# A two-block network kernel on one Trainium2 core: the scan's helper work is placed elsewhere, and the odd layer's half exchange goes from TensorE to DMA

## The chip, the core and the metric

The kernel runs on one core of a Trainium2 chip. The core has four engines that compute: TensorE (PE in the profile, its weight loads are PEld), VectorE (DVE), ScalarE (ACT) and GpSimd (POOL). SyncE (SP) issues most transfers. Each engine runs its own instructions in order and waits on semaphores for the others. The metric is the time of one execution on the device in microseconds (us).

## What is computed

The reference runs a first network of two layers (feed-forward blocks around two mixers), and then a second one of an even and an odd layer, on 512 latent tokens and 256 context tokens of width 1024, all in float32. The change touches two places of the second network. In the even layer a recurrence runs over the tokens, forwards and backwards, in 12 heads of 64:

```python
def step(s, inp):
    r_t, w_t, k_t, v_t, kk_t, b_t = inp
    sa = jnp.einsum('bhij,bhj->bhi', s, kk_t)
    s = s * w_t[:, :, None, :] - sa[..., None] * b_t[:, :, None, :] + v_t[..., None] * k_t[:, :, None, :]
    return s, jnp.einsum('bhij,bhj->bhi', s, r_t)
```

In the odd layer q and k of each of 8 heads of width 128 are turned by a position-dependent angle, which pairs feature d with feature d + 64:

```python
t1, t2 = t[..., :half], t[..., half:]
return jnp.concatenate([t1 * cos - t2 * sin, t1 * sin + t2 * cos], axis=-1)
```

## The kernel before, in words

Activations lie with features on the partitions and tokens in the free dimension (768 columns: 512 latent, 256 context). Weights come in chunks of 512 KB by SP; ACT makes a rounded copy of each (`w_hi`, L258), GpSimd the rest (`w_lo`, L266), and TensorE multiplies with both (L303).

**The even scan** (`even_scan_phase`). The 12 heads are done two at a time, in 6 blocks. A block has 6 steps, one for each 128 tokens, and a step does both directions d = 0 and 1. For each 128 tokens the recurrence is turned into products with a triangular 128x128 matrix that must be inverted. Three kinds of work run at once, all placed by hand in the in-order programs of the engines:

- The *step* of block b: `chunk_parts` (`take`, `keys`, `cross`, `join`, `turn`, `close`, for the step to come) and `state_parts` (`right`, `solve`, `read`, `write`, for this step). DVE masks and adds (`br`, `kqr`, `y`, `x`, then `add`, L2884 to L2891), ACT copies out of PSUM. ACT's first copy of a step is `bq` (L2681); its start marks the step in this document.
- The *inversion* of block b+1: its diagonal 32x32 blocks are gathered by DMA to 96 partitions, and GpSimd runs 30 rounds of substitution (`invert`, L2321 to L2331). ACT then writes a turned (transposed) copy in two pieces, L2667 for the first 21 columns and L2671 for the rest. SP writes both forms to DRAM (`scatter`, L2236 and L2239) and reads them back as `image` (L2259), which `cross` of the block needs (L2455).
- The *preparation* of block b+2: from the projected rows it makes the decays, their powers, and their products with r, k and so on (`prepare` on each engine).

Preparation and inversion are cut into slots: a block has 36, six in each step, and `between(slot)` in a step places slot n = 6k + slot (first the inversion's part, then the preparation's). The slots that matter: the reciprocals of the key norm `inv` (128 columns each, L2805) stand at n = 9 to 14; ACT's powers at n = 17 to 26; the turned copies at n = 25 and 27; DVE's `rk` (L2824) at n = 28; DVE's copy of the last decay column and its product with the row r (`last`, L2829, and `r`, L2832) at n = 29 and 30; `bonus` (L2837), which waits for `r1`, at n = 32; the lower triangles for the inversion (`low`, PE L2420, DVE L2940) at n = 33, 34, 35 and at 0, 1, 2 of the next block. GpSimd does the inversion of c and then the ten products of the preparation of c+1 (L2338): `kk`, `ksum`, `bkk0`, `b0`, `q0`, `bkk1`, `b1`, `q1`, `kw0`, `kw1`; `kk` waits for `inv`. Blocks 0 and 1 are prepared ahead of the first step, the others inside steps: blocks 0 to 3 of steps hold a preparation, block 4 holds only the inversion of block 5, and block 5 holds nothing. Where blocks are numbered below it is the block whose steps run, from 0 to 5, and steps are 0 to 5 too.

**The odd layer** (`odd_phase`). For each head h TensorE does `project(h, Q)`, `turn_values(h-1)`, `project(h, KEY)`, `rotate(h, Q)`, `turn_keys(h-1)`, `project(h, V)`, `rotate(h, KEY)`, `products(h-1)`, `project(h-1, G)`, `outputs(h-1)`. ACT copies each result out (`evacuate`: `plain` for q and k, L3304 and L3309), and `project(h, V)` waits for the copy of KEY, since both use the bank `con`. `rotate` (L3426) is a product with a 128x128 matrix of 0, 1 and -1 that swaps the halves. DVE's `turn` then forms plain x cos + rotated x sin in three operations (L3535, L3536, L3538). `products` and `outputs` wait for ACT and DVE in their turn.

## Time and profile before

| | us |
|---|---|
| median of 3 runs | 3448.47 |
| lowest, highest | 3445.60, 3452.94 |
| the profiled execution | 3458.49 |
| its span, first to last instruction | 3456.7 |
| PE busy | 3143.7 (91%) |
| DVE, ACT, GpSimd busy | 1642.9, 1177.2, 1317.2 |
| mean granted TensorE clock | 0.945 |
| the scan's steps, first to last | about 2440 to 2902 |
| the odd layer | about 3043 to the end |

The span is the time from the first to the last instruction of one profiled execution; the time outside it is 1.8 us. Busy shares are means over the whole program. What an edit is worth is read from the stage in which it stands.

### The profile page before, as it was taken

How to read it: one execution, taken by the hardware profiler on the slowest of the kernel's cores; microseconds unless marked ns; L12 is line 12 of the kernel's file. 1: busy time of each engine (PE TensorE's matmuls, PEld its weight loads, DVE VectorE, ACT ScalarE, POOL GpSimd, SP SyncE). 2: the span in 40 equal slices, each digit the busy share in tenths (PEclk: the TensorE clock that was granted, in tenths of full speed). 3: DMA queues.
4: the chain of work that ended last, by engine and by line, in shares of the span. 5: the costliest groups of instructions: out<-in, count | busy, mean ns of one | idle time of the engine just before them, and what ended most of it. 6: DMA issues, size and time to landing. Idle time of an engine off the chain costs nothing. (4 is left out here: it accounts for less than half of the span.)

```text
span 3456.7 us, 51217 instructions
## 1 busy us (share of the span) xinstructions
PE 3143.7 (91%) x19551; PEld 2512.9 (73%) x19551; DVE 1642.9 (48%) x3075; ACT 1177.2 (34%) x2107; POOL 1317.2 (38%) x863
## 2 busy tenths in 40 slices
PE   6999989799998999989899989996788889979996
PEld 5888865588886888767688867874566666758875
DVE  6444377344535573332531115426777755264443
ACT  2222235322223222234322223234444434243342
POOL 3444431344443434333344432224666630133332
PEclk8999989899998999989899999997899999979998
DMA  7565421265544554322333332222222233112111
GB/s 228 180 188 165 133 66 48 74 194 184 165 155 129 179 167 140 110 74 62 119 109 95 96 94 85 63 93 64 47 54 55 55 104 108 37 54 62 56 49 43
DMA packets 633361, 361.15 MB, mean 104 GB/s; under 512 B 106830, under 2 KB 626756, under 8 KB 632672
## 3 DMA queue, kind: packets, MB, share of 16 engines
q1 hardware_dynamic: 628960, 351.48, 34.3%
q10 hardware_dynamic: 3056, 6.29, 0.5%
q8 instruction: 124, 2.03, 0.2%
q0 software_dynamic: 1168, 0.91, 0.1%
q14 instruction: 53, 0.43, 0.0%
HBM read 333.73 MB, written 24.90 MB: 104 GB/s over the span
## 5 line engine op out<-in xcount | busy, mean ns | idle before, releaser
L266 POOL TENSOR_TENSOR w_lo<-w_raw,w_hi 128x1024 fp32r<-128x1024 f32 (+1 forms) x398 | 940.4, 2364 | 1731.9 <-ACT w_hi L258 1731.9
L303 PE MATMUL acc<-h,w_hi 128*128 128x512 f32 x3136 | 979.0, 393 | 6.7 <-POOL w_lo L266 6.7
L258 ACT ACTIVATE w_hi<-w_raw 128x1024 fp32r<-128x1024 f32 (+1 forms) x398 | 414.5, 1042 | 989.2 <-PE acc L303 961.0
L303 PEld LDWEIGHTS acc<-h,w_hi 128*128 128x128 f32 x3136 | 584.2, 188 | 128.6 <-POOL w_lo L266 7.8
L303 PE MATMUL acc<-h,w_lo 128*128 128x512 f32 x1568 | 613.4, 391 | 0.0
L303 PE MATMUL acc<-hid,w_hi 128*128 128x512 f32 x1408 | 437.3, 392 | 0.0
L303 PE MATMUL lat<-h,w_hi 128*128 128x512 f32 x912 | 336.6, 408 | 19.6 <-DVE h L429 17.6
L303 PEld LDWEIGHTS acc<-h,w_lo 128*128 128x128 f32 x1568 | 294.9, 188 | 63.6
L830 DVE SCALAR_TENSOR_TENSOR ada_part<-ada_raw,c_act,ada_part 128x256 f32<-128x256 f32 x672 | 314.9, 488 | 18.6
L303 PEld LDWEIGHTS acc<-hid,w_hi 128*128 128x128 f32 x1408 | 263.7, 188 | 54.2
L303 PE MATMUL acc<-hid,w_lo 128*128 128x512 f32 x704 | 275.2, 391 | 0.0
L1162 DVE TENSOR_TENSOR prod<-sil,acc 128x512 f32<-128x512 f32 x88 | 60.5, 688 | 420.1 <-ACT sil L1074 400.7
L303 PEld LDWEIGHTS lat<-h,w_hi 128*128 128x128 f32 x912 | 172.7, 192 | 66.0 <-issue 13.4
L353 DVE TENSOR_TENSOR ssq<-ssq,sq 128x512 f32<-128x512 f32 (+1 forms) x41 | 44.4, 1084 | 301.2 <-ACT sq L455 270.3
L303 PE MATMUL con<-h,w_hi 128*128 128x256 f32 x656 | 186.0, 284 | 0.0
L303 PE MATMUL lat<-h,w_lo 128*128 128x512 f32 x456 | 183.0, 401 | 0.0
L303 PEld LDWEIGHTS acc<-hid,w_lo 128*128 128x128 f32 x704 | 132.5, 188 | 28.0
L303 PEld LDWEIGHTS con<-h,w_hi 128*128 128x128 f32 x656 | 125.4, 191 | 0.1
L1165 DVE TENSOR_TENSOR hid<-prod,hid 128x512 f32 (+1 forms) x88 | 67.8, 771 | 81.6 <-ACT hid L1076 81.6
L2058 DVE SCALAR_TENSOR_TENSOR u<-lat,mods,u 128x504 f32 (+1 forms) x80 | 56.7, 708 | 99.7 <-ACT u L1962 96.7
L303 PEld LDWEIGHTS lat<-h,w_lo 128*128 128x128 f32 x456 | 87.4, 192 | 22.0
L323 PE MATMUL acc<-h,w_hi 128*128 128x512 f32 x192 | 71.4, 457 | 23.1 <-DVE h L570 23.1
(517 smaller groups left out, 4844.5 us busy)
## 6 DMA issues: line engine op xcount, KB each, us to landing
w_raw<-in_ffn_w SPq DMA_DIRECT2D x240, 512.0 KB, 3.9
ada_raw<-in_ada_w SPq DMA_DIRECT2D x88, 1024.0 KB, 4.9
w_raw<-in_od_w_in SPq DMA_DIRECT2D x32, 512.0 KB, 4.0
w_raw<-in_ev_w_in SPq DMA_DIRECT2D x30, 512.0 KB, 3.8
w_raw<-in_ffn_w SPq DMA_DIRECT2D x32, 384.0 KB, 3.3
image<-inverse_wait SPq DMA_DIRECT2D x144, 64.0 KB, 2.1
first_ada<-in_ada_w SPq DMA_DIRECT2D x8, 1024.0 KB, 12.5
w_raw<-in_ab_w_in SPq DMA_DIRECT2D x16, 512.0 KB, 3.8
```

The source lines that it names most:

```text
L258: act.activation(K.w_hi[:, first % SPLIT, 0:tiles, :], K.raw[:, first % RAW, 0:tiles, :], ACT.Copy).then_inc(K.hi_ready, 1)
L266: pool.tensor_tensor(K.w_lo[:, first % SPLIT, 0:tiles, :], K.raw[:, first % RAW, 0:tiles, :], K.w_hi[:, first % SPLIT, 0:tiles, :].bitcast ...
L303: mm = pe.matmul(out, w[:, slot, k, :], moving(ap, k, tokens), start=first and k == 0 and p == 0, stop=last and k == tiles - 1 and p == le ...
L323: mm = pe.matmul(outs[c], w[:, (n + c) % SPLIT, kc, :], moving(ap, kc, LAT), start=kc == 0 and p == 0, stop=kc == DB - 1 and p == len(PASS ...
L353: dve.tensor_tensor(K.ssq[:, 0:width], K.ssq[:, 0:width], K.sq[:, b % 2, 0:width], ALU.add).then_inc(N.ssq_added, 1)
L830: ins = dve.scalar_tensor_tensor(out, raw[:, k, :], col, part[:, v, :], ALU.mult, ALU.add)
L1162: dve.tensor_tensor(prod[:, s % 2, :], sil[:, s % 2, :], banks[2 * (s % 2) + 1][:], ALU.mult).then_inc(S.prod_ready, 1)
L1165: dve.tensor_tensor(hid[:, LO, at(i, 1), :], prod[:, s % 2, :], hid[:, HI, at(i, 1), :].bitcast(F32), ALU.subtract).then_inc(S.hid_ready, 1)
L2058: dve.scalar_tensor_tensor(dst, src, col, dst, ALU.mult, ALU.add).then_inc(S.shifted, 1)
```

## The change

In the scan:

- The turned copies move from n = 25 and 27 to n = 20 and 23 (for all blocks but the first).
- `r0` and `r1` go from DVE to GpSimd: for the blocks 2 to 5 behind `q0`, for the blocks 0 and 1 behind `q1`. `last0` and `last1` go from DVE to ACT, both at n = 28. ACT's powers stand one slot later (24 to 27). `bonus` waits for GpSimd's `r1`.
- For the blocks 2 to 5 the six reciprocals stand at n = 9, 10, 11, 19, 21 and 22 (9 to 14 before), and `inv` is signalled at the last of them.

In the odd layer the 16 matrix products are gone. Behind the copy-out and the split of q and of k, ACT waits for its own copy and issues two DMAs that write the upper half of `plain` to the lower half of `swapped` and the other way round; DVE waits for their landing, and its first operation now reads SBUF where it read PSUM. The sign is in the table `rope`, and the 64 KB load of `rot` is gone.

```diff
 PREP = {
-    "act": [..., "q0", "q1", "w0", "w1"],
-    "dve": ["kk", "max", "sum0", "inv", "sum1", ..., "before1", "rk", "last0", "r0", "last1", "r1", "bonus"],
-    "pool": ["kk", "ksum", "bkk0", "b0", "q0", "bkk1", "b1", "q1", "kw0", "kw1"],
+    "act": [..., "q0", "q1", "w0", "w1", "last0", "last1"],
+    "dve": ["kk", "max", "sum0", "sum1", ..., "before0", "inv", "before1", "rk", "bonus"],
+    "pool": ["kk", "ksum", "bkk0", "b0", "q0", "r0", "r1", "bkk1", "b1", "q1", "kw0", "kw1"],
...
+                        if d == (c < 2):
+                            for e in range(2):
+                                op(f"r{e}", O.cs[e], O.cs[e], reads, ALU.mult, ("act", f"last{e}"))
...
+                        if n == 28:
+                            act.wait_ge(S.pa, prep("act", c, f"w{d}"))
+                            t = 0 if d else CH - 1
+                            act.activation(O.wlast[:, d, :], O.cs[d].rearrange("p (c t) -> p c t", t=CH)[:, :, t],
+                                           ACT.Copy).then_inc(S.pa, 1)
...
-                    if c and n == 25:
+                    if c and n == 20:
                         act.wait_ge(S.solving, c * (2 * N - 2) + 2 * early)
...
-                    if n == (27 if c else 17):
+                    if n == (23 if c else 17):
                         act.wait_ge(S.solved, c + 1)
...
+                    places = (9, 10, 11, 19, 21, 22) if c > 1 else range(9, 15)
...
                     if n == 32:
-                        own("r1")
+                        dve.wait_ge(S.pq, prep("pool", c, "r1"))
...
                     split(n + SPLIT)
+                    if kind in (Q, KEY):
+                        act.wait_ge(S.evac, n + 1)
+                        for to, of in ((slice(0, 64), slice(64, 128)), (slice(64, 128), slice(0, 64))):
+                            act.dma_start(swapped[kind][to], halves(plain[of, kind, :])).then_inc((S.q_swapped, S.k_swapped)[kind], 16)
...
-                    rotate(h, Q)
...
-                    rotate(h, KEY)
...
-                    dve.wait_ge(S.rot_ps, 2 * h + kind + 1)
+                    dve.wait_ge((S.q_swapped, S.k_swapped)[kind], 32 * h + 32)
...
-                    steps(dve.tensor_tensor(part[:], rot_ps[:], rope[:, 1, :], ALU.mult))
+                    part = swapped[kind]
+                    steps(dve.tensor_tensor(part, part, halves(rope[:, 1, :]), ALU.mult))
```

Where the order of instructions moves, three places. On DVE at the join of step 4 and step 5 of a block with a preparation (`state` ends step 4; `br` and `kqr` are `take` and `keys` of step 5), before:

```order
L2891 SCALAR_TENSOR_TENSOR state<-gathered,w_last,const 128x128
L2824 SCALAR_TENSOR_TENSOR x_context<-x_context,params,u 128x768
L2829 COPY w_last<-q_r_rate 128x6
L2832 TENSOR_TENSOR q_r_rate<-q_r_rate,u 128x768
L2848 TENSOR_TENSOR br<-chunk_479,masks 128x256
L2848 TENSOR_TENSOR br<-chunk_493,masks 128x256
L2829 COPY w_last<-q_r_rate 128x6
L2832 TENSOR_TENSOR q_r_rate<-q_r_rate,u 128x768
L2855 TENSOR_TENSOR kqr<-chunk_479,masks 128x512
```

and after:

```order
L2892 SCALAR_TENSOR_TENSOR state<-gathered,w_last,const 128x128
L2833 SCALAR_TENSOR_TENSOR x_context<-x_context,params,u 128x768
L2849 TENSOR_TENSOR br<-chunk_479,masks 128x256
L2849 TENSOR_TENSOR br<-chunk_493,masks 128x256
L2856 TENSOR_TENSOR kqr<-chunk_479,masks 128x512
```

The four instructions of `last` and `r` between the step's own are gone. On ACT at the end of step 3 of such a block (`sa` is `solve`, `t` and `y` are `turn` and `close`, `q_r_rate` a power, `bq` opens step 4), before:

```order
L2711 ACTIVATE sa<-state_494 128x128
L2689 ACTIVATE t<-chunk_479 64x2x64
L2692 ACTIVATE y<-chunk_479 64x128
L2689 ACTIVATE t<-chunk_493 64x2x64
L2692 ACTIVATE y<-chunk_493 64x128
L2698 ACTIVATE t<-chunk_479 64x2x64
L2698 ACTIVATE t<-chunk_493 64x2x64
L2623 ACTIVATE q_r_rate<-q_r_rate 128x768
L2681 ACTIVATE bq<-chunk_479 128x256
```

and after:

```order
L2718 ACTIVATE sa<-state_494 128x128
L2674 ACTIVATE w_raw<-w_raw 96x32x21
L2696 ACTIVATE t<-chunk_479 64x2x64
L2699 ACTIVATE y<-chunk_479 64x128
L2696 ACTIVATE t<-chunk_493 64x2x64
L2699 ACTIVATE y<-chunk_493 64x128
L2705 ACTIVATE t<-chunk_479 64x2x64
L2705 ACTIVATE t<-chunk_493 64x2x64
L2678 ACTIVATE w_raw<-w_raw 96x32x11
L2688 ACTIVATE bq<-chunk_479 128x256
```

The two pieces of the turned copy (`w_raw`) came from behind the `sa` of step 4; the second stands ahead of the `bq` of step 4 now. In block 4, which has no preparation, the order is the same without the power. On ACT in the odd layer, from the copy-out of q to that of k (`v_tok` and `k_zeta` are tokens of the head before, `var` and `m` belong to the output of the one before that), before:

```order
L3304 ACTIVATE plain<-lat_631 128x512
L258 ACTIVATE w_hi<-w_raw 128x1024
L3322 ACTIVATE v_tok<-factors_498 128x512
L3326 ACTIVATE v_tok<-factors_499 128x256
L3329 ACTIVATE k_zeta<-factors_499,zeta 128x128 x4
L3350 ACT_TABLE_LOAD
L3350 ACTIVATE var<-var 128x512
L3354 ACTIVATE m<-sq 128x512
L3308 ACTIVATE k<-con 128x256
L3309 ACTIVATE plain<-lat_632 128x512
```

and after:

```order
L3303 ACTIVATE plain<-lat_631 128x512
L254 ACTIVATE w_hi<-w_raw 128x1024
L3321 DMA swapped<-plain 64x512 x2
L3325 ACTIVATE v_tok<-factors_498 128x512
L3329 ACTIVATE v_tok<-factors_499 128x256
L3332 ACTIVATE k_zeta<-factors_499,zeta 128x128 x4
L3353 ACT_TABLE_LOAD
L3353 ACTIVATE var<-var 128x512
L3357 ACTIVATE m<-sq 128x512
L3307 ACTIVATE k<-con 128x256
L3308 ACTIVATE plain<-lat_632 128x512
```

The row of the two DMAs is new there; two more stand behind the split that follows the copy-out of k.

## Rows read from the trace of the kernel before

**Rows 1.** Windows: start:end length, busy PE PEld DVE ACT POOL, clock, DMA share, GB/s.
```profile
2823.10:2833.30 10.20, 9.85 (x168) 7.73 (x167) 5.44 (x16) 5.89 (x18) 4.97 (x14) 1.00 0.25 39
2833.30:2849.20 15.90, 11.79 (x169) 9.29 (x167) 5.54 (x16) 3.84 (x17) 0.00 (x0) 0.89 0.39 76
...
3131.70:3321.80 190.10, 188.40 (x1070) 159.23 (x1070) 87.48 (x100) 73.42 (x121) 62.97 (x30) 1.00 0.20 56
```

**Rows 2.** Windows: steps 4 and 5 together, of blocks 0 to 3.
```profile
2493.90:2526.50 32.60, 26.84 (x363) 21.02 (x361) 23.98 (x42) 11.85 (x38) 18.84 (x10) 0.84 0.28 57
2579.80:2611.40 31.60, 24.16 (x362) 18.70 (x361) 23.94 (x42) 11.83 (x37) 18.88 (x10) 0.95 0.29 59
2665.00:2696.90 31.90, 25.44 (x362) 19.97 (x361) 23.86 (x43) 11.85 (x38) 18.20 (x9) 0.89 0.26 54
2750.10:2780.30 30.20, 24.22 (x363) 18.57 (x361) 23.89 (x42) 11.84 (x38) 18.82 (x10) 0.94 0.30 62
```

**Rows 3.** Timeline (start, length, instruction, wait), DVE and PE, block 2, step 5.
```profile
2675.73 1.78 DVE L2829 COPY w_last<-q_r_rate 128x6 f32<-128x6 f32 x1
2677.55 2.52 DVE L2832 TENSOR_TENSOR q_r_rate<-q_r_rate,u 128x768 f32<-128x768 f32 x1
...
2680.65 1.11 DVE L2829 COPY w_last<-q_r_rate 128x6 f32<-128x6 f32 x1
2681.79 2.52 DVE L2832 TENSOR_TENSOR q_r_rate<-q_r_rate,u 128x768 f32<-128x768 f32 x1
...
2684.96 1.29 PE L2455 MATMUL chunk<-image,bq 64*64 64x64 f32 x16 [2.76 <-DVE kqr L2855]
```

**Rows 4.** Timeline of GpSimd, block 2: preparation behind the inversion.
```profile
2662.87 1.82 POOL L2338 TENSOR_TENSOR x<-x,x_context 128x768 f32<-128x768 f32 x1 [0.18 <-POOL w_raw L2329]
...
2671.08 3.65 POOL L2338 TENSOR_TENSOR q_r_rate<-q_r_rate,x 128x768 f32<-128x768 f32 x2
...
2677.44 1.80 POOL L2338 TENSOR_TENSOR q_r_rate<-q_r_rate,x 128x768 f32<-128x768 f32 x1
```

**Rows 5.** One line's instructions (min/median/max ns, first to last): DVE's reciprocals.
```profile
L2805 DVE RECIPROCAL x_context<-x_context x36: 893/935/954, 2322.6 to 2730.6; 128x128 f32<-128x128 f32 x36
```

**Rows 6.** Timeline of ACT and PE, block 4: steps 4 and 5.
```profile
2823.08 0.38 ACT L2681 ACTIVATE bq<-chunk 128x256 f32<-128x256 f32 x1 [1.38 <-PE chunk L2439]
...
2829.18 0.82 ACT L2671 ACTIVATE w_raw<-w_raw 96x352 f32<-96x352 f32 x1 [1.11 <-POOLq L2331]
...
2839.84 0.45 PE L2455 MATMUL chunk<-image,bq 64*64 64x64 f32 x8 [3.15 <-DMA image<-inverse_wait]
```

**Rows 7.** Timeline of GpSimd, DVE and PE just ahead of block 0.
```profile
2427.94 1.79 POOL L2338 TENSOR_TENSOR q_r_rate<-q_r_rate,x 128x768 f32<-128x768 f32 x1
...
2430.58 1.02 DVE L2837 TENSOR_TENSOR u<-prep,u 128x512 f32<-128x512 f32 x2
...
2431.75 1.23 PE L2420 MATMUL prep<-q_r_rate 64*128 64x128 f32 x8 [7.86 <-DVE u L2837]
```

**Rows 8.** Timeline of ACT and PE, odd layer, one head: KEY to V.
```profile
3254.78 0.63 ACT L3354 ACTIVATE m<-sq 128x512 fp32r<-128x512 f32 x1 [4.94 <-DVE sq L3573]
...
3255.51 1.02 PE L3426 MATMUL rot<-plain,rot 128*128 128x512 f32 x2
...
3255.99 0.59 ACT L3309 ACTIVATE plain<-lat 128x512 f32<-128x512 f32 x1
...
3256.37 0.60 PE L3454 MATMUL factors<-const,k 128*128 128x128 f32 x4
...
3256.72 0.47 PE L303 MATMUL lat<-h,w_hi 128*128 128x512 f32 x1
```

**Rows 9.** ACT behind a DMA issue; its landing (us, last); PE, head 1.
```profile
2309.59 1.06 ACT L258 ACTIVATE w_hi<-w_raw 128x1024 fp32r<-128x1024 f32 x1 [0.46 <-ACT late L1885]
...
late_wait<-late ACTq DMA_DIRECT2D x10, 384.0 KB, 2.3
...
3104.61 0.47 PE L303 MATMUL lat<-h,w_hi 128*128 128x512 f32 x1 [1.45 <-ACT plain L3309]
```

More of the change, by code:

```diff
@@ L157, in constants @@
     cos, sin = np.cos(ang), np.sin(ang)
-    rope = np.stack([np.concatenate([cos, cos]), np.concatenate([sin, sin])]).astype(np.float32)
-    rot = np.zeros((P, P), np.float32)
-    for d in range(half):
-        rot[half + d, d] = -1.0
-        rot[d, half + d] = 1.0
+    rope = np.stack([np.concatenate([cos, cos]), np.concatenate([-sin, sin])]).astype(np.float32)
     posrow = np.stack([np.broadcast_to(i + 1.0, (P, P)), np.broadcast_to(P - i + 0.0, (P, P))])
@@ L166, in constants @@
         "dft_feat": feat.astype(np.float32), "dft_ctx": time[0], "dft_lat": time[1],
-        "rope": rope, "rot": rot, "posrow": posrow.astype(np.float32),
+        "rope": rope, "posrow": posrow.astype(np.float32),
     }
@@ L2080 @@
     "pe": ["norm", "decay0", "decay1", "rate0", "rate1", "bonus"],
[3 rows of a table removed]
-}
[3 rows of a table added]
+}
+PREP_FIRST = dict(PREP, dve=["kk", "max", "sum0", "inv", "sum1", "kt0", "kt1", "k0", "k1", "before0", "before1", "rk", "bonus"],
+                  pool=["kk", "ksum", "bkk0", "b0", "q0", "bkk1", "b1", "q1", "r0", "r1", "kw0", "kw1"])
 SUBBLOCK = 32
@@ L2166, in prep @@
         def prep(engine, c, name):
[L2168 removed]
+            return c * len(PREP[engine]) + ((PREP if c > 1 else PREP_FIRST)[engine].index(name) + 1)
         def blocks(prepare, invert, low, begin, step):
@@ L2340, in prepare @@
                     q, rate = O.q, O.rate
+                    reads = u[:, c:c + 1, :].rearrange("p a t -> p (a t)")
                     op("kk", kk, kk, tmp, ALU.mult, ("dve", "inv"))
@@ L2752, in _ @@
                 late(1)
-                for n in range(17, 25):
+                for n in range(17, 26):
                     prepare(0, n)
                 late(2)
-                for n in range(25, NCH * SLOTS):
+                for n in range(26, NCH * SLOTS):
                     prepare(0, n)
@@ L2801, in prepare @@
                         done(dve.tensor_scalar(tmp, tmp, 1e-12, None, ALU.max))
-                    if 9 <= n < 15:
+                    places = (9, 10, 11, 19, 21, 22) if c > 1 else range(9, 15)
+                    if n in places:
                         own("max")
-                        sl = slice((n - 9) * CH, (n - 8) * CH)
+                        part = places.index(n)
+                        sl = slice(part * CH, part * CH + CH)
                         inverse = dve.reciprocal(tmp[:, sl], tmp[:, sl])
+                        if part == NCH - 1:
+                            done(inverse)
                     if 11 <= n < 15:
                         sums((n - 11) % 2, (n - 11) // 2)
-                    if n == 14:
-                        done(inverse)
                     for d in range(2):
@@ L2824, in prepare @@
                         done(dve.scalar_tensor_tensor(tmp, tmp, col("r_k"), row(0), ALU.mult, ALU.mult))
-                    for d in range(2):
-                        if n == 29 + d:
-                            act(f"w{d}")
-                            t = 0 if d else CH - 1
-                            done(dve.tensor_copy(O.wlast[:, d, :], O.cs[d].rearrange("p (c t) -> p c t", t=CH)[:, :, t]))
-                        if n == 29 + d:
-                            own(f"last{d}")
-                            done(dve.tensor_tensor(O.cs[d], O.cs[d], row(0), ALU.mult))
                     if n == 32:
-                        own("r1")
+                        dve.wait_ge(S.pq, prep("pool", c, "r1"))
                         dve.wait_ge(S.pp, prep("pe", c, "bonus"))
@@ L3211, in odd_phase @@
     with phase(K, *norm_names("pre"), *norm_names("post"), *SUB_SEMS, "tables", "logits", "decay_tables", "lg", "steps",
-               "decays", "made", "evac", "rot_ps", "rot_read", "roped", "turned", "turn_copied", "sc_ps", "sc_ready",
+               "decays", "made", "evac", "q_swapped", "k_swapped", "rot_read", "roped", "turned", "turn_copied", "sc_ps", "sc_ready",
                "kv_ps", "states", "xi_ready", "o_ps", "o_copied", "sum_ps", "var", "std", "inv", "m_full", "m_hi",
@@ L3223, in odd_phase @@
         rope = S.sb("rope", [P, 2, SEQ])
-        rot = S.sb("rot", [P, P])
         plain = S.sb("plain", [P, 2, SEQ])
-        part = S.sb("part", [P, SEQ])
+        halves = lambda ap: ap.rearrange("p (a t) -> p a t", a=2)
+        swapped = (halves(S.sb("swapped", [P, SEQ])), K.sq[:, :, SEQ:TOK])
         q = S.sb("q", [P, 2, SEQ])
@@ L3260, in _ @@
                 sp.dma_start(rope[:], A["rope"].rearrange("m p t -> p m t")).then_inc(S.tables, 16)
-                sp.dma_start(rot[:], A["rot"]).then_inc(S.tables, 16)
                 sp.dma_start(lg[:, 5, :], A["od_decay_logit_2"].rearrange("a d h -> a (d h)").broadcast_to(
@@ L3420, in project @@
                              before=(lambda k: pe.wait_ge(S.h_ready, k + 1)) if n == 0 else None)
-                def rotate(h, kind):
-                    pe.wait_ge(S.evac, number[h, kind] + 1)
-                    if h or kind:
-                        pe.wait_ge(S.rot_read, 2 * h + kind)
-                    pe.matmul(rot_ps[:], rot[:], plain[:, kind, :], start=True, stop=True).then_inc(S.rot_ps, 1)
                 def piece(t, h, c):
@@ L3481, in sums @@
                     pe.matmul(R[1][:], K.ones, K.ssq[:], start=True, stop=True).then_inc(S.sum_ps, 1)
-                pe.wait_ge(S.tables, 32)
                 for h in range(HEADS):
@@ L3525, in _ @@
                         "spread")
-                dve.wait_ge(S.tables, 32)
+                dve.wait_ge(S.tables, 16)
                 def turn(h, kind):
                     dst = (q, k)[kind][:, h % 2, LAT]
-                    dve.wait_ge(S.rot_ps, 2 * h + kind + 1)
+                    dve.wait_ge((S.q_swapped, S.k_swapped)[kind], 32 * h + 32)
                     if h >= 2:
```

8 lines of the change are left out of this document (3 added, 5 removed), and 4 rows, old and new, of the table PREP.

## The prediction

> **What bounds the kernel now.** I read the windows first, to see which stages the change touches and what is busy there; then the waits and the timeline of the scan's longest steps; then the timeline of one head of the odd layer. The chain of waits of the page covers only the last microseconds and says nothing on these stages.
>
> A step of block 4 with nothing but the last of an inversion in it takes 10.2 us, of which PE is busy 9.85 [rows 1]: a bare step is bound by PE and by short hand-overs. Of the steps that hold a preparation, 4 and 5 are the longest pair: together 32.6, 31.6, 31.9 and 30.2 us in the four blocks [rows 2], 31.6 in the mean, where two bare steps are 20.4. In them DVE is busy 24 us of 32, and the preparation's work stands ahead of the step's: in step 5 `last` and `r` take 1.78 + 2.52 us, then comes `br`, then they take 1.11 + 2.52 us, and only then comes `kqr`, for which PE waits 2.76 us [rows 3]. The granted clock of these windows is 0.84 to 0.95 [rows 2] against 1.00 in the bare step [rows 1]; PE had idled just before it fell.
>
> The odd layer's steady part has PE busy 188.4 of 190.1 us at clock 1.00 [rows 1]. It is bound by PE, or by what stands just behind it.
>
> **Scan, `last` and `r` off DVE (blocks 0 to 3).** The four instructions are 1.78 + 2.52 + 1.11 + 2.52 = 7.9 us of DVE [rows 3], all on the path of step 5. They are not 7.9 us of gain, for PE is next: the four windows hold 24.2 to 26.8 us of PE, the larger ones at the lower clock [rows 2]. At full clock I put PE's work at 23.5 us. Above that stand the hand-overs, which in a bare step are 0.35 us (10.2 less 9.85), so 0.7 for two, and the three `low` products of step 5, where PE waits in turn for DVE's mask: some 2 us (an estimate). That is a floor of about 26. The new load of GpSimd gives back something: two products at 1.82 us each [rows 4] make its preparation 3.6 us longer, so that it now overlaps nearly all of step 5. I take 27 us for the pair, against 31.6: **-4.5 us a block, -18 in all**. Bounds: 25.6 (-24 in all) and 29.6 (-8).
>
> The row for the giving back: a product of 768 columns on DVE took 2.52 us, from 2677.55 to 2680.07 [rows 3]; a GpSimd product ran from 2677.44 to 2679.24 [rows 4], and DVE was done 0.83 us behind its end. The Trainium skill (SBUF — State Buffer, Who interferes with whom) states that a DVE instruction with two SBUF inputs and a GpSimd one exclude each other for their whole length. By that rule the two `state` updates in step 5 can each wait up to one GpSimd product, so the pair would be up to 3.6 us longer in each block and the scan's gain -3.6 instead of -18; this pair of rows agrees with the rule. GpSimd worked through most of step 5 before the change too, so I count little of it.
>
> ACT takes `last` at n = 28 behind its powers, two copies of six columns, where the turned copies (the second piece alone 0.82 us [rows 6]) leave step 4: nothing on the path. `r0` waits for it. GpSimd's `r1`: `kk` starts at 2662.87 in block 2, the inversion having just ended [rows 4]; with `inv` now signalled at the end of step 3 I put it 1.2 us later. The two products from 2671.08 on are `q0` and `bkk1` [rows 4], so `q0` ended at 2672.9 and now ends at 2674.1, `r1` at 2677.8. `bonus` would be reached in step 5 about 3.5 us behind the step's start of 2675.9, so near 2679. It fits by little more than a microsecond; a late `r1` would hold DVE and behind it `x`, `state` and the `low` masks.
>
> **Scan, the reciprocals.** Three of 0.94 us [rows 5] leave step 2 and come into step 3. Step 2 is bound by DVE and gains 2.8; step 3 has small slack on DVE (some 0.5 us) and pays 2.3. Less PE idling in step 2 may help the clock there and hurt it in step 3. Sum **0**, bounds -3 and +4 over four blocks.
>
> **Scan, the turned copy.** In blocks 0 to 3 it stands at the end of step 3, where the inversion has just ended (2662.87 less 0.18 [rows 4]; step 4 starts at 2665.0). The power that stood at n = 23 has moved on and makes room. The images come earlier, but PE does not wait for them there. **0**. In block 4 steps are bare, and the inversion ends late: ACT's second copy had to wait for it until 2829.18 although it stood in the middle of step 4 [rows 6]. Now it stands ahead of `bq` of step 4, which was at 2823.08 [rows 6]: ACT is held until 2829.18 + 0.82 = 2830.0, and step 4 starts 6.9 us late. The copy is no earlier than before, so the images land no earlier, at 2839.84. But step 5 then reaches `cross` near 2843 and waits no more; it lost 15.9 - 10.2 = 5.7 us before [rows 1]. Net 6.9 - 5.7 = 1.2, and PE idles twice as long at a stretch, which costs clock: **+2 us** (0 to +5).
>
> **Ahead of block 0.** `bonus` of block 1 ran at 2430.58, and PE waited 7.86 us for it [rows 7]. Now it waits for `r1`, behind `q1`, which ended at 2427.94 + 1.79; without DVE's products in its way 0.5 earlier, 2429.2; two products of 1.82: 2432.8. **+2.3 us** (+1 to +3). `kw0` and `kw1` move later behind it, and the first steps do not need them.
>
> **Odd layer.** A rotation holds PE 3256.37 - 3255.51 = 0.86 us [rows 8], 16 of them 13.8. They do not all come back. Behind `rotate(h, Q)` and the 0.35 us of `turn_keys` stands `project(h, V)`, at 3256.72, and it needs the copy of KEY, which ended at 3255.99 + 0.59 = 3256.58 [rows 8]: that rotation was covered but for 0.14. And ACT gets longer just there. An issue put 0.46 us between two of its instructions [rows 9]; two stand between the copy of q and the value tokens, some 0.8 us, and I let a short wait of ACT for PE take 0.25 of it. All behind it, `var`, DVE's reciprocal and `m` (ending at 3255.41 [rows 8]) move by 0.55, to 3255.96. The copy into `k` ahead of `plain` stood at 3255.7, so it starts 0.25 later, and V starts 0.25 us *later* than before. The rotation of KEY, between V and `products`, comes back whole: what `products` waits for was ready long before. So a steady head gives 0.86 - 0.25 = 0.6 us; seven KEY rotations give 6.0, six heads of the other kind cost 1.5. Heads 0 and 1 are tied to ACT (PE waited 1.45 us for it at 3104.61 [rows 9]); there the rotation of KEY of head 0 no longer holds DVE's decay tables up, and with ACT's issues I put it at -1.6. Sum **-6 us**. Bounds: -13.8 if every rotation comes back, and +1 if an issue pair holds ACT for 1.6 us.
>
> The transfers themselves: a landing took 2.3 us [rows 9]; DVE uses q and k more than 5 us after, behind its other work. The first of `turn`'s operations now reads SBUF twice. Covered: PE needs the result only one projection later.
>
> **The sum.** -18 + 0 + 2 + 2.3 - 6 = -19.7. The profiled execution was 3458.5 and would be 3438.8; it lay 10 us above the median of the three runs, so for the median 3448.5 - 19.7 = **3429 us**.
>
> **Rivals.** (a) *The exchange frees all it removed, and the pair comes down to PE's floor*: ACT's issues fall into its waits. For it: ACT is busy 73 of 190 us there [rows 1]. Against it: the rows that follow each other from q's copy to k's. 3448.5 - 13.8 - 24 + 4.3 = 3415. (b) *GpSimd and DVE hold each other up*: the pair gives 2 us a block only. For it: 2.52 against 0.94. 3448.5 - 8 + 4.3 - 6 = 3439. The rule above is this rival; by its full length it would be 3443. (c) *The changes in the scan do nothing, since steps 4 and 5 are bound by PE at the low clock*: PE busy 26.8 of 32.6 at 0.84 [rows 2]. Against it: the waits for DVE come ahead of the low clock. Gain 0 there: 3448.5 + 4.3 - 6 = 3447. (d) *Slower: GpSimd's `r1` is the new end of step 5.* It is ready 1.2 us ahead of `bonus` by my count. Each microsecond it is late holds DVE, and with it `x` and the `low` masks, in four blocks. From 6 us late on, 4 x 6 = 24 us have eaten the gain; at 9 us late it is 3429 + 36 = 3465. Against it: GpSimd would need some 23 us for the seven products to `r1`, and two took 3.65 [rows 4].
>
> **Chances.** The forecast 0.53, (a) 0.17, (b) 0.19, (c) 0.07, (d) 0.04. The median of this kernel can be told from no change from about 0.2% on, 7 us. Faster by more than that, under 3441.6: the forecast, (a) and most of (b), 0.87. Within: 0.09. Slower: 0.04. The range that should hold 8 in 10 leaves out (c), (d) and the far half of (a): 3412 to 3442.
>
> **What would show it.** Right: the two steps 4 and 5 of block 2 together near 27 us, with no `last` or `r` row on DVE and PE's wait for `kqr` under 1 us; step 2 shorter and step 3 longer by the same; ACT waiting some 7 us for the inversion's end in block 4, step 3, and no wait for `image` in step 5; a wait of PE for `plain` ahead of each V of about 1 us, and none for `swapped`; a head at 37.4 us for 38.0. Wrong: `bonus` waiting for GpSimd; `state` rows over 1 us in step 5; a head at 36.3 (rival a) or over 38.

## The result, and the profile after the change

The changed kernel's median is 3431.0 us (four runs, 3429.75 to 3433.30). The kernel before, run beside it, is at 3450.7 us (3445.60 to 3455.39). The ratio is 0.9945, 95% interval 0.9931 to 0.9959: 19.7 us less. The prediction was 3429.0, or 19.7 us less than its own median of before. In a later comparison on another occasion the changed kernel was at 3436.79 against 3448.87 (ratio 0.9955, 0.9943 to 0.9968), so the gain is 12 to 20 us by two comparisons, and in both it is more than the 0.2% (7 us) from which on a change can be told.

The profiled executions have spans of 3456.7 and 3431.5 us, 25.2 apart. 5.8 of these lie ahead of the scan's first step, in code that the change does not touch. The rest divides as follows. Steps are marked by the start of ACT's first `bq`, heads of the odd layer by the start of ACT's copy of `gates`, in both traces.

| part | before | after | difference | predicted |
|---|---|---|---|---|
| ahead of block 0 (wait for `bonus`) | 30.2 | 32.3 | +2.2 | +2.3 |
| steps 4 and 5, blocks 0 to 3 | 126.2 | 106.5 | -19.7 | -18 |
| step 2, blocks 0 to 3 | 66.6 | 56.9 | -9.7 | -11 |
| step 3, blocks 0 to 3 | 43.2 | 49.0 | +5.8 | +9 |
| steps 0 and 1, blocks 0 to 3 | 104.6 | 107.7 | +3.1 | 0 |
| block 4, its six steps | 68.9 | 71.6 | +2.7 | +2 |
| odd layer, six steady heads | 228.2 | 222.7 | -5.4 | -3.7 |
| odd layer, first heads and the rest | | | +1.8 | -2.3 |

The predicted -11 and +9 are the prediction's 2.8 and 2.3 us for four blocks; in its sum it booked the two together as 0.

Windows of the changed kernel, the columns of [rows 1]. First the four pairs of steps 4 and 5, which answer to [rows 2]:

```profile
2489.71:2516.27 26.56, 23.57 (x362) 18.17 (x361) 18.30 (x39) 10.75 (x38) 22.51 (x12) 0.97 0.35 72
2568.98:2596.26 27.28, 24.29 (x362) 18.77 (x361) 18.29 (x39) 10.74 (x38) 22.50 (x12) 0.94 0.38 78
2649.91:2675.75 25.84, 22.84 (x362) 17.77 (x361) 18.30 (x39) 10.76 (x39) 22.50 (x12) 1.00 0.33 67
2729.32:2756.10 26.78, 24.15 (x362) 18.76 (x361) 17.76 (x38) 10.97 (x39) 21.49 (x12) 0.93 0.36 70
```

DVE is busy 18 us in place of 24, GpSimd 22.5, and the pair takes 26.6 us in the mean for 31.6.

Then block 4, steps 3, 4 and 5, and five steady heads of the odd layer, which answer to [rows 1]:

```profile
2788.91:2805.58 16.67, 11.22 (x193) 8.72 (x191) 5.65 (x16) 6.04 (x19) 13.61 (x28) 0.97 0.01 2
2805.58:2817.52 11.94, 10.27 (x141) 8.22 (x142) 5.48 (x16) 3.86 (x17) 0.00 (x0) 0.75 0.63 110
2817.52:2827.65 10.13, 9.87 (x168) 7.67 (x167) 5.44 (x16) 3.81 (x16) 0.00 (x0) 1.00 0.13 30
3138.65:3324.25 185.60, 181.01 (x1052) 155.84 (x1051) 77.62 (x100) 74.09 (x120) 59.49 (x29) 1.00 0.25 69
```

Step 3 is now the long one, step 4 runs at clock 0.75 behind it, and step 5, which took 15.9 us in [rows 1], takes 10.1 like any bare step. A head takes 37.12 us for 38.03.

The timeline of ACT at the end of block 4's step 3 (start, length, instruction, idle before it and what ended that): the second turned copy waits 6.87 us for the inversion's end, where [rows 6] had 1.11.

```profile
2804.76 0.80 ACT L2678 ACTIVATE w_raw<-w_raw 96x352 f32<-96x352 f32 x1 [6.87 <-POOLq L2329]
```

The timeline of DVE in block 2 around the start of step 5 (2660.63), which answers to [rows 3], and of GpSimd there, which answers to [rows 4]:

```profile
2659.52 2.57 DVE L2833 SCALAR_TENSOR_TENSOR x_context<-x_context,params,u 128x768 f32<-128x768 f32 x1
2662.01 0.74 DVE L2849 TENSOR_TENSOR br<-chunk,masks 128x256 f32<-128x256 f32 x2
2664.44 1.29 DVE L2856 TENSOR_TENSOR kqr<-chunk,masks 128x512 f32<-128x512 f32 x2 [1.69 <-PE chunk L2448]
...
2666.49 1.01 DVE L2838 TENSOR_TENSOR u<-prep,u 128x512 f32<-128x512 f32 x2
...
2670.11 1.08 DVE L2892 SCALAR_TENSOR_TENSOR state<-gathered,w_last,const 128x128 f32<-128x128 f32 x1
```

```profile
2657.59 1.86 POOL L2336 TENSOR_TENSOR q_r_rate<-q_r_rate,x 128x768 f32<-128x768 f32 x1
2659.41 4.34 POOL L2336 TENSOR_TENSOR q_r_rate<-q_r_rate,u 128x768 f32<-128x768 f32 x2
2663.72 1.82 POOL L2336 TENSOR_TENSOR q_r_rate<-q_r_rate,x 128x768 f32<-128x768 f32 x1
```

No `last` and no `r` stands on DVE. DVE now waits for PE ahead of `kqr`, and PE no longer waits for `kqr` (2.76 us before). GpSimd's `r0` and `r1` (2659.41, two) are ready at 2663.75, 2.7 us ahead of `bonus` (2666.49), which waits for nothing. But `rk` (L2833) takes 2.57 us and the first `state` 1.08. Before, in the same block, they took:

```profile
2674.80 1.00 DVE L2824 SCALAR_TENSOR_TENSOR x_context<-x_context,params,u 128x768 f32<-128x768 f32 x1
...
2692.37 0.35 DVE L2891 SCALAR_TENSOR_TENSOR state<-gathered,w_last,const 128x128 f32<-128x128 f32 x1
```

The same instruction has two durations. That is the thread of what follows.

Ahead of block 0, DVE, which answers to [rows 7]; PE waits 10.03 us there for 7.86:

```profile
2426.95 1.02 DVE L2838 TENSOR_TENSOR u<-prep,u 128x512 f32<-128x512 f32 x2 [11.91 <-POOL q_r_rate L2336]
```

### The profile page after: what moved, and what is told of

Same layout as the page of the kernel before. It is cut to its first block and busy times, and to the rows that moved or that the text cites. A ratio compares the mean times of both kernels' runs of the same rounds, so it can differ in the third digit from the quotient of the medians.

```text
span 3431.5 us, 51169 instructions
## 1 busy us (share of the span) xinstructions
PE 3121.0 (91%) x19519; PEld 2497.9 (73%) x19519; DVE 1591.0 (46%) x3051; ACT 1180.3 (34%) x2119; POOL 1330.3 (39%) x875
## 5 line engine op out<-in xcount | busy, mean ns | idle before, releaser
L299 PE MATMUL acc<-h,w_hi 128*128 128x512 f32 x3136 | 978.9, 393 | 6.6 <-POOL w_lo L262 6.6
L299 PE MATMUL lat<-h,w_hi 128*128 128x512 f32 x912 | 334.5, 407 | 25.3 <-DVE h L425 19.0
L299 PEld LDWEIGHTS lat<-h,w_lo 128*128 128x128 f32 x456 | 87.6, 192 | 19.9
L299 PE MATMUL con<-h,w_lo 128*128 128x256 f32 x328 | 93.5, 285 | 0.0
```

The costliest lines, as they stand in the source:

```text
L299: mm = pe.matmul(out, w[:, slot, k, :], moving(ap, k, tokens), start=first and k == 0 and p == 0, stop=last and k == tiles - 1 and p == le ...
```

## Experiments

Ratios and differences are of medians, against the kernel before in the same comparison: 3452.08 us for the first four kernels, 3450.94 for the next four, 3448.87 for the last four.

### The exchange alone, and the rows alone

The kernel before with the odd layer's hunks of the diff and nothing else:

> The kernel before with the odd layer's exchange alone. By the two traces a steady head is 37.12 us for 38.03, and the gain is all in the rotation of KEY (0.86) while V starts only 0.04 earlier behind KEY; six such heads give 5.4. Heads 0 and 1 and the tail ran 0.9 and 0.6 us longer at a lower granted clock, which need not come again. Theory: -4 to -6 us against the kernel before, V waiting 0.57 us for the copy `plain` in each head. The prediction's term was -6 with V starting 0.25 later. Rival (a), every rotation comes back: -13.8. Rival, the transfers cost something elsewhere: 0.

Measured: 3445.44 us, -6.6, ratio 0.9977 (0.9967 to 0.9988). By the interval the exchange is worth 4 to 11 us. The six heads took 222.7 us, as in the changed kernel, so 5.4 us are the steady heads. From the scan's last step to the first `gates` it was 2.2 us shorter than before, where the changed kernel's trace had 1.1 more. But 1.5 of the 2.2 lie ahead of the odd layer's first product, where the two kernels do the same work; heads 0 and 1 are taken up again below.

The kernel before with `last` on ACT and `r` on GpSimd and nothing else:

```diff
-    "dve": [..., "rk", "last0", "r0", "last1", "r1", "bonus"],
+    "dve": [..., "rk", "bonus"],
-    "pool": [..., "q0", "bkk1", "b1", "q1", "kw0", "kw1"],
+    "pool": [..., "q0", "r0", "r1", "bkk1", "b1", "q1", "kw0", "kw1"],
...
+                        if n == 28:
...
+                            act.activation(O.wlast[:, d, :], ...)
```

> The kernel before with one edit: `last` on ACT at n = 28, `r0` and `r1` on GpSimd. Turned copies, powers and reciprocals stay as before. Theory: steps 4 and 5 of blocks 0 to 3 are 26.6 us in the mean for 31.6 (-4.9 each, -19.7), PE ahead of block 0 waits 2.2 us longer for `bonus`: -17.5 us against the kernel before, step 2 still 16.7 us at granted clock 0.90. Rival: part of the pair's gain belongs to the reciprocals and the turned copies that left these steps; then the pair stays above 28.5 us and the whole is -10 or less. Rival (b), GpSimd and DVE hold each other up: -6.

Measured: 3435.68 us, -16.4, ratio 0.9944 (0.9931 to 0.9958). The pairs are 29.0, 26.0, 27.3 and 27.6 us, 27.5 in the mean. Two of its pairs, blocks 0 and 1:

```profile
2492.01:2521.05 29.04, 25.30 (x362) 19.40 (x361) 19.14 (x38) 12.01 (x40) 22.95 (x15) 0.90 0.34 72
2574.65:2600.64 25.99, 22.76 (x362) 17.76 (x361) 19.00 (x40) 12.02 (x40) 21.23 (x12) 1.00 0.34 68
```

The same 362 products, 3 us apart: PE is busy 25.3 us at clock 0.90 and 22.8 at 1.00. This one edit carries nearly all of the scan's gain: from the `bq` ahead of block 0 to the scan's last step it is 466.3 us, 464.0 in the changed kernel and 479.7 before.

### What GpSimd does to the step when nothing leaves DVE

This was meant to price rival (b): the kernel before, plus two products on GpSimd that nobody needs.

```diff
-    "pool": [..., "q1", "kw0", "kw1"],
+    "pool": [..., "q1", "again0", "again1", "kw0", "kw1"],
...
+                        op(f"again{e}", kk, kk, kk, ALU.mult, ...)
```

> The kernel before, with two more products of 768 columns on GpSimd behind `q1` of each preparation (kk by itself, whose value nothing reads afterwards), all else as before: GpSimd's load of the change without any gain of it. Theory: GpSimd and DVE hardly hold each other up; steps 4 and 5 stay at 30 to 32 us a block, and the whole within 2 us of the kernel before. Rival (b) and the rule that the two exclude each other for a whole instruction: DVE's state updates and products in step 5 are up by one GpSimd product for each, +1.8 to +3.6 us a block, +7 to +14 in all.

Measured: 3440.37 us, **-10.6**, ratio 0.9969 (0.9957 to 0.9981). More work on GpSimd made the kernel faster, which neither the theory nor the rival expected. Block 2, step 5 of that kernel, DVE and then GpSimd:

```profile
2665.46 0.76 DVE L2831 COPY w_last<-q_r_rate 128x6 f32<-128x6 f32 x1
2666.26 0.96 DVE L2834 TENSOR_TENSOR q_r_rate<-q_r_rate,u 128x768 f32<-128x768 f32 x1
```

```profile
2664.14 4.41 POOL L2338 TENSOR_TENSOR x<-x 128x768 f32<-128x768 f32 x2
```

The second `r` took 0.96 us where it took 2.52 in [rows 3]. It got in 0.02 us ahead of GpSimd's second extra product (the two start at 2666.26 and 2666.28), and here GpSimd waited: its product took 2.27 us for 1.80. It is the same in all four blocks, where `r` starts 0.01 to 0.02 us ahead each time. The durations of [rows 3] are thus not DVE's work. GpSimd's products in the kernel before, in that step:

```profile
2674.87 2.61 POOL L2338 TENSOR_TENSOR q_r_rate<-q_r_rate,w_inv 128x768 f32<-128x768 f32 x1
2677.44 1.80 POOL L2338 TENSOR_TENSOR q_r_rate<-q_r_rate,x 128x768 f32<-128x768 f32 x1
2679.21 2.52 POOL L2338 TENSOR_TENSOR x<-x,x_context 128x768 f32<-128x768 f32 x1
2681.69 1.80 POOL L2338 TENSOR_TENSOR x<-x,w_inv 128x768 f32<-128x768 f32 x1
```

The first `last` of [rows 3] (1.78 us) ends with the product that ends at 2677.48; `r` (2677.55) is done 0.83 us behind the one that ends at 2679.24; GpSimd's next one, started at 2679.21, is itself 0.7 us longer than its neighbours (2.52 for 1.80), having to let `r` finish; the second `last` ends 0.03 us behind it; the second `r` again 0.8 us behind the next. They take turns, one instruction at a time. The Trainium skill (SBUF — State Buffer, Who interferes with whom) has this: a DVE instruction with two SBUF inputs, or a copy in its two-port mode, and a GpSimd instruction that reads SBUF hold one pair of ports exclusively for their length, and the order of issue decides who blocks. The rows before the change agree, in both directions and to 0.1 us. That the copy of 128x6 is held up they show; in which mode it ran they do not.

The test, which takes nothing off DVE and only keeps GpSimd away while the second pair runs:

```diff
-op(f"kw{d}", O.kt[d], O.kt[d], wi[d], ALU.mult, ("pool", "ksum"))
+op(f"kw{d}", O.kt[d], O.kt[d], wi[d], ALU.mult, ("dve", "r1"))
```

> The kernel before with one wait other: GpSimd's `kw0` and `kw1` wait for DVE's `r1` of the same preparation. Nothing leaves DVE. In the trace of before, DVE's `last` and `r` of block 2's step 5 end with a GpSimd product or 0.83 us behind one's end (1.78, 2.52, 1.11, 2.52 us); in the kernel with two more GpSimd products the last two took 0.76 and 0.96 us and that kernel was 10 us faster than before. Theory: DVE's own work in the four is 2.3 us and the rest is waiting for GpSimd to let go of SBUF; with `kw` out of the way the second `last` takes 0.2 and the second `r` 0.95 us, the pair of steps 4 and 5 is 28.5 to 29.5 us for 31, and the kernel is -6 to -11 us against before. Rival: 2.5 us is what a product of 768 columns takes on DVE there, whatever GpSimd does, and the gain of the other kernel was chance of the clock: the rows stay at 2.52 and the whole at 0.

Measured: 3437.09 us, -11.8, ratio 0.9962 (0.9949 to 0.9975); pairs 29.1, 29.0, 27.3 and 29.9, 28.8 in the mean. DVE, then GpSimd, block 2, step 5:

```profile
2661.60 1.78 DVE L2829 COPY w_last<-q_r_rate 128x6 f32<-128x6 f32 x1
2663.42 2.52 DVE L2832 TENSOR_TENSOR q_r_rate<-q_r_rate,u 128x768 f32<-128x768 f32 x1
...
2666.52 0.15 DVE L2829 COPY w_last<-q_r_rate 128x6 f32<-128x6 f32 x1
2666.71 0.96 DVE L2832 TENSOR_TENSOR q_r_rate<-q_r_rate,u 128x768 f32<-128x768 f32 x1
```

```profile
2660.74 2.62 POOL L2338 TENSOR_TENSOR q_r_rate<-q_r_rate,w_inv 128x768 f32<-128x768 f32 x1
2663.32 1.80 POOL L2338 TENSOR_TENSOR q_r_rate<-q_r_rate,x 128x768 f32<-128x768 f32 x1
2667.75 1.81 POOL L2338 TENSOR_TENSOR x<-x,x_context 128x768 f32<-128x768 f32 x1 [2.63 <-DVE q_r_rate L2832]
```

The same two instructions, 1.78 + 2.52 us beside GpSimd and 0.15 + 0.96 alone, the latter in all four blocks. Of the 7.9 us in the prediction's term, 2.2 were DVE's work and 5.7 were waiting inside the instructions. In block 2 PE waits 0.4 us for `kqr` in place of 2.8, and the pairs are 2.7 us shorter. One changed wait gives more than half of the gain of the rows (11.8 of 16.4 by the medians, 11.0 of 16.3 in the traces' pairs). The clock moved too: PE is busy 23.7 us of a pair for 25.2, at granted clocks of 0.94 to 1.00 for 0.84 to 0.95. What part of the gain came through it, the experiment does not tell.

A third sight of it is in the trace of the exchange alone, whose scan is that of before. In its block 2, step 3 took 13.6 us (it fell into a stretch of low clock), so GpSimd was further on when step 5 began (its last product ended at 2676.46, just ahead of the first `r`), and the pair took 26.5 us at clock 1.00, while that of the block before took 33.2 at 0.85. DVE there:

```profile
2672.23 2.56 DVE L2820 SCALAR_TENSOR_TENSOR x_context<-x_context,params,u 128x768 f32<-128x768 f32 x1
2674.71 1.77 DVE L2825 COPY w_last<-q_r_rate 128x6 f32<-128x6 f32 x1
2676.52 0.96 DVE L2828 TENSOR_TENSOR q_r_rate<-q_r_rate,u 128x768 f32<-128x768 f32 x1
...
2678.06 0.16 DVE L2825 COPY w_last<-q_r_rate 128x6 f32<-128x6 f32 x1
2678.25 0.96 DVE L2828 TENSOR_TENSOR q_r_rate<-q_r_rate,u 128x768 f32<-128x768 f32 x1
```

### How late may GpSimd be?

The changed kernel with `r0` and `r1` behind `q1` in every block (`if d:` for `if d == (c < 2):`):

> The changed kernel, with `r0` and `r1` on GpSimd behind `q1` in every block, three products (5.4 us) later. In the changed kernel's block 2 `r1` ended 2.7 us ahead of `bonus`. Theory (the prediction's rival d as a mechanism): `bonus` now waits for GpSimd some 2.7 us in each of blocks 0 to 3 and holds DVE's queue behind it, so steps 4 and 5 are up by that: +11 us against the changed kernel. Rival: the work queued in front of PE covers the wait, as DVE has slack in step 5 now: 0 to +4.

Measured: 3435.56 us, -15.4 against before, ratio 0.9953 (0.9940 to 0.9966). The changed kernel's own two medians are 3431.0 and 3436.8, so this median cannot be told from it; the trace says more. DVE, block 2:

```profile
2658.50 1.01 DVE L2833 SCALAR_TENSOR_TENSOR x_context<-x_context,params,u 128x768 f32<-128x768 f32 x1
...
2666.53 1.02 DVE L2838 TENSOR_TENSOR u<-prep,u 128x512 f32<-128x512 f32 x2 [1.26 <-POOL q_r_rate L2336]
```

`bonus` waits 1.28, 2.53, 1.26 and 2.53 us in the four blocks, 7.6 in all, and the pairs are 27.4 us in the mean, 0.8 above the first trace of the changed kernel and 0.2 above the second. The theory's 11 is wrong: in blocks 0 and 2 `rk` now meets no product of GpSimd and takes 1.0 us again, and PE has other work while DVE waits (it stands idle for 0.7 of the 1.3 us, and for 2.0 of the 2.5). The rival had the size.

### The reciprocals

The changed kernel with the reciprocals back at n = 9 to 14 (`places = range(9, 15)`):

> The changed kernel, with the six reciprocals back in slots 9 to 14 in every block, rows and turned copies as changed. In the traces, steps 1 to 3 of blocks 0 to 3 summed 163.4 us in the changed kernel, and 165.1 in the kernel with the rows alone: spread reciprocals shorten step 2 (14.1 to 14.4 us for 15.2 to 16.6), lengthen step 3 by 1.1, and a stretch of low clock moves from step 2 into step 1 or 3. Theory: the spread is worth little, 0 to 3 us, so this kernel is 0 to +3 against the changed one, step 2 back at 15.2 to 16.6. Rival: spreading the reciprocals is what keeps the clock up in steps 2 to 5; without it +6 or more. Rival: it costs (GpSimd starts `kk` later behind it): -3.

Measured: 3431.72 us, -19.2 against before; the changed kernel was -19.7 and -12.1 in its two comparisons. Step 2 is 15.3, 15.3, 16.7 and 15.2 us, 5.6 more in all than in the changed kernel's trace; step 1 gives back 3.6 and the other steps another 2. The spread of the reciprocals is worth nothing that can be told.

### The turned copies of the last inversion

```diff
-if c and n == 20:
+if c and n == (25 if c == RB - 1 else 20):
...
-if n == (23 if c else 17):
+if n == ((27 if c == RB - 1 else 23) if c else 17):
```

> The changed kernel, with the two turned copies of the last inversion (in block 4) back at n = 25 and 27. Theory: ACT is no longer held for the inversion's end at the start of step 4; step 3 goes from 16.7 to 10.4 us and step 4 from 11.9 to 10.2, and PE's wait for `image` in block 4's step 5 comes back (10.1 to 15.9): 2.3 us less than the changed kernel. Rival: the position makes no difference, since the chain from the inversion's end to the images is the same: 0. Rival: the copies in the step's middle start the images later than ahead of it: +1.

Measured: 3428.44 us, -23.6, ratio 0.9931 (0.9918 to 0.9945). Block 4, steps 3 and 5:

```profile
2791.63:2801.95 10.32, 9.87 (x168) 7.67 (x167) 5.63 (x16) 3.82 (x16) 9.11 (x16) 1.00 0.02 4
...
2812.18:2828.25 16.07, 12.72 (x168) 9.99 (x167) 5.54 (x16) 3.81 (x16) 0.00 (x0) 0.79 0.38 75
```

The three steps sum to 36.6 us for 38.7: 2.1 less, where the theory had 2.3. The images' chain is indeed the same, and holding ACT for it costs more than letting PE wait at its end. The total of 2.6 less than the changed kernel's first median is less than the changed kernel's two medians differ by (5.8); the trace carries this one.

### ACT's issues and the V product

The odd layer in the changed kernel, one steady head, ACT and then PE. They answer to [rows 8]; L3321 is the issue:

```profile
3221.05 0.60 ACT L3303 ACTIVATE plain<-lat 128x512 f32<-128x512 f32 x1 [4.39 <-PE lat L299]
3221.55 1.05 ACT L254 ACTIVATE w_hi<-w_raw 128x1024 fp32r<-128x1024 f32 x1
3221.68 1.14 ACTq L3321 DMA_DIRECT2D swapped<-plain  x2
3222.87 0.60 ACT L3325 ACTIVATE v_tok<-factors 128x512 f32<-128x512 f32 x1 [0.27 <-issue]
3223.36 0.38 ACT L3329 ACTIVATE v_tok<-factors 128x256 f32<-128x256 f32 x1
```

```profile
3233.55 0.47 PE L299 MATMUL lat<-h,w_hi 128*128 128x512 f32 x1 [0.57 <-ACT plain L3308]
```

The two issues take 1.14 us, but 0.92 of it runs beside the split `w_hi`. The first copy of the value tokens is 1.82 us behind q's copy for 1.44 before, and the second 2.31 for 2.30, because before it waited 0.27 us for PE. Nothing behind it moves. V then waits 0.57 us for `plain`, which is what the rotation of Q had covered. In the steady heads nothing waits for `swapped`, and DVE's first operation of `turn` takes 0.68 us for 0.69.

Each exchange as four transfers of 32 partitions:

> The changed kernel, each exchange of halves as four transfers of 32 partitions in place of two of 64: the same bytes, twice the issues on ACT. In the changed kernel the first copy of the value tokens starts 1.82 us behind q's copy for 1.44 before, but the second, which had waited 0.27 us for PE, is where it was (2.31 and 2.30): the pair of issues costs 0.38 us of ACT and the wait takes it. Theory: two issues more are not covered; the second copy, the root of var and DVE's reciprocal come 0.4 to 0.9 us later, V's wait for `plain` grows, and a steady head goes from 37.1 to 37.4 to 37.9 us, 2 to 6 us in all. Rival: ACT has more slack, as it is busy under half of the head: head unchanged, 0.

Measured: 3440.77 us, -8.1, ratio 0.9976 (0.9968 to 0.9985), 4.0 more than the changed kernel in the same comparison. The six heads took 227.8 us for 221.8. ACT and PE:

```profile
3223.90 2.50 ACTq L3321 DMA_DIRECT2D swapped<-plain  x4
3226.44 0.60 ACT L3325 ACTIVATE v_tok<-factors 128x512 f32<-128x512 f32 x1 [1.63 <-PE factors L3440]
```

```profile
3236.72 0.47 PE L299 MATMUL lat<-h,w_hi 128*128 128x512 f32 x1 [1.52 <-ACT plain L3308]
```

The two issues more are 1.36 us, all of it beyond the cover, and come out as 1.0 us of each head. So the prediction's mechanism exists, and the pair of issues just fits in the slack.

V waiting for the context copy of KEY alone, which ACT makes ahead of `plain` and which alone shares V's bank (`con_read` is signalled by that copy):

```diff
-pe.wait_ge(S.evac, number[h, KEY] + 1)
+pe.wait_ge(S.con_read, h + 1)
```

> The changed kernel, with PE's V product of each head waiting for the copy of the context part of KEY (which shares its PSUM bank) and no longer for `plain`, which ACT makes behind it. Theory: the wait of 0.57 us ahead of each V is the copy `plain` and nothing stands behind it, so a steady head goes from 37.12 to 36.6 us and the kernel loses 8 x 0.57 = 4.6 us against the changed kernel, perhaps 1.5 more if the low clock at V of head 1 goes too. Rival: the chain through var, its reciprocal and m on ACT and DVE is the next bound just there, and the head stays at 37.1: 0.

Measured: 3432.18 us, -19.9, ratio 0.9938 (0.9925 to 0.9952). The head is 36.63 us, V waits 0.08 us in place of 0.57, and PE is busy for all but 0.43:

```profile
3119.10:3155.73 36.63, 36.20 (x212) 31.16 (x211) 15.52 (x21) 14.82 (x24) 12.39 (x7) 1.00 0.27 73
```

In the trace the six heads are 2.9 us shorter than in the changed kernel's first trace and 2.0 than in its second. The theory's 4.6 is not in the median, which is 1.2 above the changed kernel's first, with runs from 3425.1 to 3433.7.

### The composed kernel

Last turned copies back, V behind the context copy, and `last` and `r` of the preparations of blocks 0 and 1 on DVE as before:

> The changed kernel with three edits: the last inversion's turned copies back at n = 25 and 27; V waiting for the context copy of KEY alone; `last` and `r` of the preparations of blocks 0 and 1 back on DVE. Theory: -2.2 (block 4), -3.9 to -6 (odd layer), -2.2 (`bonus` ahead of block 0, whose wait goes from 10.0 back to 7.9 us): -8 to -10 against the changed kernel, some 3422 us. Rival: part of it is taken by stretches of lower clock, which have come and gone by 2 us a block between kernels with equal code: -4.

Measured: 3421.54 us (3418.42 to 3428.82), -29.4, ratio 0.9918 (0.9905 to 0.9930): faster than both kernels. In its trace the stretch ahead of block 0 is 30.15 us for 32.33, block 4 68.4 for 71.6, the steady head 36.63 for 37.12. That is 2.2, 3.2 and (for six heads) 2.9 us, 8.3 in all, where the theory had 8 to 10; the median is 9.5 below the changed kernel's first.

The same with the reciprocals back too:

> The composed kernel (last turned copies back, V behind the context copy alone, rows of blocks 0 and 1 on DVE) with the reciprocals back in slots 9 to 14 too. Theory: by the earlier pair the spread of the reciprocals is worth 0 to 1 us, so this is 3421.5 within 2. Rival: with the other edits in, step 2 (62.6 for 57.3 us in four blocks) is no longer given back by steps 1, 3 and 5: +4.

Measured: 3428.33 us, -20.5, ratio 0.9935 (0.9917 to 0.9952), its six runs lying from 3414.0 to 3432.8. Its interval overlaps the composed kernel's. In the traces its scan is 3.8 us longer, as the rival had it (step 2 longer by 7.8 in four blocks, step 3 shorter by 4.2). Whether the kernel is slower is open.

The changed kernel once more:

> The changed kernel once more, to have its time and a second trace of it beside the others of this call: 3431 us, within 3, the scan's pairs within 1 us of the first trace and the odd layer's steady head at 37.0 to 37.1 us.

Measured: 3436.79 us (3429.19 to 3440.91), -12.1. That is 2.8 us beyond the range expected (3428 to 3434). The scan took 467.4 us for 464.0, the pairs 27.2 for 26.6; the heads 36.96 for 37.12. The scan's differences go with the clock: block 0's step 1 is 13.3 us here and 15.3 in the first trace, its step 3 13.6 and 11.9.

## The prediction, step by step

**The size of the whole** was right, 19.7 us, and so was the mean pair (26.6 for 27). That it came out to the tenth is luck: the rows of the table miss by up to 4 us either way and cancel, and the same kernel gave 12.1 in its second comparison. The next points show which terms were right for reasons that did not hold.

**`last` and `r` off DVE.** The step that failed is "the four instructions are 7.9 us of DVE". They are 2.2 us of work and 5.7 of waiting for GpSimd. The prediction quoted the rule and a pair of rows that agrees with it, and used them only for what the new load might cost, not for what the old rows contained. The gain was capped by PE's floor, so the number held. Freeing the second `last` and `r` of their waits alone brings the pair to 28.8 us; taking the 5.4 us of DVE that the four instructions still last there off it as well brings 27.5, only 1.3 more. The cap is real: at clock 1.00 a pair with PE busy 22.8 us takes 25.8 to 26.0 us, where the prediction's floor was 26 (with 23.5 us of PE where 22.8 stand).

**The giving back** was put at next to nothing and is not: `rk` takes 2.57 for 1.00 us in all four blocks, and the two `state` updates of step 5 take 1.08 and 0.75 for 0.35 us in blocks 0 to 2: 2.7 us of DVE in each of these blocks, 1.6 in block 3. Not all of it is the price of the new load: `rk` took 2.57 us also in three blocks of the kernel with `kw` behind `r1`, where GpSimd has no more work than before, and the first `state` of step 4 went the other way, from 1.81 to 0.85 us in blocks 0 and 1. The mark set for "wrong", `state` rows over 1 us, is there (1.08), with a pair of 25.8 us. It was no mark of the outcome, since DVE has room now, and such rows stood in step 4 before. Rival (b) had the mechanism and not its price.

**Slack of `r1`** was put at 1.2 us and was 2.7 us in block 2. `r1` ended 13.8 us behind the start of step 4, where the prediction had 12.8; but `bonus` started 16.6 behind it and not 14, because `kqr` ahead of it waits 1.69 us for PE and `rk` is longer. Rival (d) charged one for one; 7.6 us of waits made the pairs 1 to 3 us longer in all.

**Reciprocals:** step 2 -2.4 (predicted -2.8), step 3 +1.4 (+2.3), and not foreseen, steps 0 and 1 +0.8 a block. Steps 1 and 2 of block 0, before and after:

```profile
2452.90:2466.50 13.60, 12.61 (x180) 9.20 (x179) 8.96 (x21) 8.38 (x23) 10.97 (x24) 1.00 0.19 41
2466.50:2483.15 16.65, 14.01 (x191) 10.10 (x191) 14.49 (x29) 8.74 (x24) 15.00 (x22) 0.90 0.11 25
```

```profile
2448.43:2463.76 15.33, 14.25 (x180) 10.08 (x179) 10.27 (x22) 8.39 (x24) 12.53 (x26) 0.89 0.17 37
2463.76:2477.85 14.09, 12.61 (x191) 8.96 (x191) 11.01 (x24) 8.74 (x24) 12.62 (x19) 1.00 0.12 28
```

PE's 191 products take 14.0 us at 0.90 and 12.6 at 1.00, the 180 of step 1 the other way round: the stretch of the lower level moved a step ahead. Of step 2's 2.6 us, 1.4 are clock, and step 1 pays them back, here and in block 2; in block 3 step 3 does (13.5 us at 0.88 for 11.9 at 1.00 in the others). What places these stretches was not settled. Sum predicted 0, measured -0.8.

**Turned copies:** ACT's wait 6.87 (some 7), step 4 starts 6.3 us late (6.9), step 5 gains 5.7 (5.7), step 4 pays 1.7 at clock 0.75. Net +2.3 in these three steps and +2.7 in block 4 as a whole; undoing it gave back 2.1 (+2). The working was right; the experiment shows that the edit should have left out the last inversion.

**Ahead of block 0:** +2.2 (+2.3), undone by the composed kernel's third edit.

**Odd layer:** the steady head gave 0.91 us (0.61). The failed step is "some 0.8 us, and I let a short wait of ACT for PE take 0.25 of it". The pair of issues put the first copy of the value tokens back by 0.38 only, and the second, which had waited 0.27, by nothing; V starts 9.59 us behind KEY's start for 9.63, not 0.25 later, and PE's wait for `plain` is 0.57 us where some 1 was expected. The rest held: the rotation of KEY came back whole (0.86), that of Q did not. Heads 0 and 1 were put at -1.6 and gave next to nothing: from the layer's first product to the first `gates` it is 71.8 us before, 71.1 with the exchange alone, and 72.8 and 72.1 in the changed kernel's two traces. In head 1 the rotation of Q is gone, but PE now waits 1.7 to 1.9 us there for the value tokens (0.3 before), which stand behind ACT's issues, and V starts 12.5 us behind KEY for 12.1. V of head 1 then ran at a granted clock of 0.94 for 1.00 in the changed kernel's first trace, where products of 256 columns took 0.41 us for 0.28; from V to G it was 12.2 us there and 12.1 in the second trace, for 11.6 before and 10.7 with the exchange alone. Why the clock differs is open. The term was -6 and the exchange alone measured -6.6, of which the steady heads are 5.4.

**Rivals.** (a) was wrong in the odd layer, where V's wait for `plain` is the reason, and right that the pair comes down to PE's floor in the one block at full clock (25.8 us). (b) had a pair 2 us shorter, where it is 4.9. (d) is out: inside the steps `bonus` waits for nothing. (c) is out: with the rows alone the pairs fall by 4 us.
